# Hybrid decoder step on one core: token lists taken ahead of the sums, the turning and the down products; the samples' output projection stacked

## What is computed

```
z = h @ w_in                                   # four mixer branches and their gates
merged = sum_k sigmoid(gate_k) * (branch_k @ w_branch[k])
x = x + gate1 * (merged @ w_out)               # output projection
h = rmsnorm(x) * (1 + scale2) + shift2
scores = sigmoid(h @ router_w)                 # 64 experts, top 8 of each token
hg, hu = h @ e_gate[e], h @ e_up[e]            # 1024 -> 256, for each expert e
act = silu(hg) * hu * gates[:, e]
routed = sum_e act @ e_down[e]                 # 256 -> 1024
shared = (silu(h @ s_gate) * (h @ s_up)) @ s_down
x = x + gate2 * (routed + shared);  y = rmsnorm(x, final_g)
```

## Time and profile before

| what | value |
|---|---|
| median of 3 runs | 928.19 us |
| profiled execution: time, span | 926.03 us, 924.3 us |
| granted TensorE clock, mean | 0.988 |
| PE busy | 863.1 us (93% of the span) |
| DVE busy | 565.5 us (61%) |
| ACT busy | 308.5 us (33%) |
| DMA | 295.80 MB, mean 320 GB/s |
| longest group of PE | L870, 128x264, 1024 of them, 192.6 us |

### The profile page before, as it was taken

How to read it: one execution, slowest core, us unless ns; L and a number is a source line. 1 busy time by engine, 2 the same in 40 slices (tenths; PEclk the granted TensorE clock), 3 DMA queues, 4 the chain that set the end, 5 groups by cost and what they waited for, 6 DMA issues and landing times.

```text
span 924.3 us, 21357 instructions
## 1 busy us (share of the span) xinstructions
PE 863.1 (93%) x7880; PEld 647.2 (70%) x7880; DVE 565.5 (61%) x1415; ACT 308.5 (33%) x583; POOL 48.7 (5%) x89
## 2 busy tenths in 40 slices
PE   4799999999999998999898999999999999999995
PEld 2699999999999897566665556556665655665562
DVE  2557988899986667456354545446454654555455
ACT  3555444344346241122222323232222323222323
POOL 2010000000000000000000000000000000000000
PEclk9999999999999999999899999999999999999998
DMA  9985557888777628899988999999999999999911
GB/s 341 334 248 151 180 179 273 270 300 285 247 248 272 207 83 348 341 389 371 401 327 343 400 396 405 418 404 405 422 409 411 413 419 408 413 414 420 408 49 49
DMA packets 92702, 295.80 MB, mean 320 GB/s; under 512 B 7718, under 2 KB 45670, under 8 KB 67659
## 3 DMA queue, kind: packets, MB, share of 16 engines
q1 hardware_dynamic: 86139, 280.55, 79.3%
q0 software_dynamic: 6016, 13.10, 3.8%
q10 hardware_dynamic: 489, 1.33, 0.4%
HBM read 300.19 MB, written 4.14 MB: 329 GB/s over the span
## 4 chain that ended last, share of the span: by engine, by line
PE 67%; DMA 16%; DVE 8%; issue 5%; ACT 2%; SPq 0%; DVEq 0%; POOLq 0%; ACTq 0%
PE psum L870 26%; DMA xn<-h_table,idx 13%; PE psum L1310 7%; PE psum L1268 6%; PE psum L1227 5%; PE psum L874 5%; PE psum L1222 4%; PE psum L1259 3%; PE psum L913 2%; PE psum L1225 2%; PE psum L1228 2%; DMA wexp<-in_ada_w 1%; DMA wexp<-in_w_in 1%; DVE bc_r L2203 1%; PE psum L1274 1%
## 5 line engine op out<-in xcount | busy, mean ns | idle before, releaser
L870 PE MATMUL psum<-xn_r,wexp_r 128*128 128x264 f32 x1024 | 192.6, 287 | 7.5 <-DVE hT_r L1804 5.9
L870 PEld LDWEIGHTS psum<-xn_r,wexp_r 128*128 128x128 f32 x1024 | 160.5, 189 | 10.2 <-issue 7.8
L870 PE MATMUL psum<-hT_r,wexp_r 128*128 128x264 f32 x512 | 145.5, 284 | 0.0
L1766 DVE TENSOR_TENSOR wexp_r<-wexp,wexp_r 128x1024 fp32r<-128x1024 f32 x88 | 106.5, 1216 | 20.9 <-ACT wexp_r L1482 20.4
L1482 ACT ACTIVATE wexp_r<-wexp 128x1024 fp32r<-128x1024 f32 x88 | 92.3, 1054 | 60.2 <-PE psum L870 44.4
L1225 PE MATMUL psum<-wexp,mid 128*128 128x512 f32 x240 | 108.8, 599 | 0.8 <-ACT mid L1626 0.8
L2203 DVE TENSOR_TENSOR bc_r<-psum,xn_r 32x256 fp32r<-32x256 f32 (+2 forms) x140 | 67.6, 483 | 51.5 <-ACT xn_r L1659 28.2
L2188 DVE SCALAR_TENSOR_TENSOR hT<-psum,gcol,hT 128x256 f32<-128x256 f32 (+2 forms) x64 | 26.3, 411 | 116.8 <-ACT hT L1642 116.6
L870 PEld LDWEIGHTS psum<-hT_r,wexp_r 128*128 128x128 f32 x512 | 97.1, 190 | 0.1
L870 PE MATMUL psum<-wexp_r 128*128 128x264 f32 (+2 forms) x576 | 82.4, 283 | 1.4 <-DVE wexp L2014 1.4
L1225 PEld LDWEIGHTS psum<-wexp,mid 128*128 128x128 f32 x240 | 43.3, 190 | 57.6 <-issue 56.3
(11 more groups left out here) (329 smaller groups left out, 1291.0 us busy)
## 6 DMA issues: line engine op xcount, KB each, us to landing
wexp<-in_e_gate SPq DMA_DIRECT2D x64, 1024.0 KB, 8.2
wexp<-in_e_up SPq DMA_DIRECT2D x64, 1024.0 KB, 10.6
wexp<-in_e_down SPq DMA_DIRECT2D x64, 1024.0 KB, 9.7
wexp<-in_w_in SPq DMA_DIRECT2D x32, 1024.0 KB, 6.0
mid<-in_ada_w SPq DMA_DIRECT2D x8, 2048.0 KB, 9.7
wexp<-in_w_branch SPq DMA_DIRECT2D x8, 1024.0 KB, 5.4
wexp<-in_ada_w SPq DMA_DIRECT2D x14, 512.0 KB, 10.4
wexp<-in_w_out SPq DMA_DIRECT2D x4, 1024.0 KB, 5.8
```

Of the source, the lines that this page charges most:

```text
L870: last = mm(out, a[x], b[y], start=start and x == y == 0, stop=stop and x == 1)
L1766: V.tensor_tensor(as_r(low(u, q)), low(u, q), as_r(high(u, q)).bitcast(F32), ALU.subtract).then_inc(S["w_lo"], 1)
```

## The change

It makes these edits (cut to the core). The hunks are, in this order: the bank order, the banks of the sums, `mix` on PE, the turning of the second gate (`gateT`), the waits of `turn_rows`, `up` and `sums`, `last_sums`, and the bodies of PE and of DVE.

```
-        if (t, j) == (0, 1):
+        if (t, j) == (1, 0):
             out += [("h2T", 2, h) for h in range(2)]
...
+SUM_BANKS = (5, 6, 0, 5, 6, 0, 5, 0)
...
+        m_samples = poolH.rearrange(...)[:, 0:KT * (SAMPLE_TILE + NS)].rearrange("p (k m) -> p k m", k=KT)
...
+        def sum_ahead(c):
+            return max((b + 1 for b in range(c) if SUM_BANKS[b] == SUM_BANKS[c]), default=0)
...
+                if t == 2:
+                    both = psum[0:SAMPLE_TILE + NS, ...]
+                    for k in ks:
+                        if (j, h) == (0, 0):
+                            pe.wait_ge(S["m_split"], k + 1)
+                        if k:
+                            mm(out, as_r(m_samples[:, k, 0:NS]), w[1][:, k], start=False, stop=False)
+                        last = mm(both, as_r(m_samples[:, k, :]), w[0][:, k], start=(k == 0), stop=(k == KT - 1))
...
+            out = claim("gateT")
+            for c in range(KT):
+                last = turn(out[...], mod[:, 3 * D + c * P:3 * D + (c + 1) * P], NC_ROWS)
...
-                need(pe, S["sum_taken"], KT * sums)
+                need(pe, S["sum_taken"], KT * sums - 1)
...
-                        pe.wait_ge(S["sum_taken"], KT * sums_before(i, j) - 2)
+                        pe.wait_ge(S["sum_taken"], KT * sums_before(i, j))
...
-                    if c > 2:
-                        pe.wait_ge(S["sum_taken"], KT * i + c - 2)
+                    if sum_ahead(c):
+                        pe.wait_ge(S["sum_taken"], KT * i + sum_ahead(c))
...
+                down(LAST, UNROLL - 1)
                 last_sum(0, 1, 1)
-                down(LAST, UNROLL - 1)
+                turn_samples()
...
-                    up(i, j, range(4))
...
+                    if not prev:
+                        up(i, j, range(2))
...
                         token_list(0, 2)
+                        up(i, j, range(2, 4))
+                        turn_rows(0, 1, 0)
+                        up(i, j, range(4, 6))
                         token_list(0, 3)
+                        up(i, j, range(6, KT))
+                    else:
+                        up(i, j, range(4))
+                        turn_act(pi, pj)
+                        up(i, j, range(4, KT))
+                    if not last:
+                        token_list(i + 1, j)
                     if sums_at(i, j):
                         sums(i)
...
                     gated(i, j)
+                    if not last:
+                        list_out(i + 1, j)
```

More of the change, by code:

```diff
@@ L92, in jobs_of_mixer @@
         out.append(("mix", t, j))
-        if (t, j) == (0, 1):
+        if (t, j) == (1, 0):
             out += [("h2T", 2, h) for h in range(2)]
-    out += [("h2T", 0, h) for h in range(2)] + ["logit_first"] + [("h2T", MIX_ORDER[-1], h) for h in range(2)]
+    out += [("h2T", 0, h) for h in range(2)] + ["logit_first", "gateT"] + [("h2T", MIX_ORDER[-1], h) for h in range(2)]
     out += ["logit", ("shared_gate", 0), ("shared_up", 0), ("shared_gate", 1), ("shared_up", 1), "sort_turn", "sort", "slot", "order", "lists"]
@@ L1068, in mix @@
                 out = psum[0:n, bank_of(("mix", t, j))[0], h * UNIT:(h + 1) * UNIT].rearrange("p (q n) -> p q n", q=2)
+                if t == 2:
+                    both = psum[0:SAMPLE_TILE + NS, bank_of(("mix", t, j))[0], h * UNIT:(h + 1) * UNIT].rearrange("p (q n) -> p q n", q=2)
+                    for k in ks:
[4 more added lines that the diff above has]
+                        last = mm(both, as_r(m_samples[:, k, :]), w[0][:, k], start=(k == 0), stop=(k == KT - 1))
+                        if not k:
+                            last = mm(out, as_r(m_samples[:, k, 0:NS]), w[1][:, k], start=False, stop=False)
+                    return last
                 for k in ks:
-                    if (t, j, h) == (2, 0, 0):
-                        pe.wait_ge(S["m_split"], k + 1)
                     last = mm3(out, [as_r(m_hi[:, k, t0:t0 + n]), as_r(mT[:, k, t0:t0 + n])], [x[:, k] for x in w], start=(k == 0), stop=(k == KT - 1))
@@ L1100, in _ @@
             full(logits(out, MIX_ORDER[1], range(KT)), "logit_first")
+            await_freed(pe, ("ada", 11))
+            out = claim("gateT")
+            for c in range(KT):
+                last = turn(out[:, c * NC_ROWS:(c + 1) * NC_ROWS], mod[:, 3 * D + c * P:3 * D + (c + 1) * P], NC_ROWS)
+            full(last, "gateT")
             turn_h(MIX_ORDER[2])
@@ L1198, in _ @@
             await_freed(pe, ("shared_gate", 1))
[L1200 to L1205, removed]
             def up(i, j, ks):
@@ L1381, in body @@
                         down(pi, pj)
[L1382 to L1385, removed]
                     if last and j == 2:
@@ L1617, in _ @@
             scores("logit", MIX_ORDER[2:])
+            b = await_full(ac, "gateT")
+            free(F(gate_col[:], b[:, 0:KT * NC_ROWS].rearrange("p (c r) -> p c r", r=NC_ROWS)[:, :, NS], ACT.Copy), "gateT")
             def shared_silu(j):
@@ L2043, in _ @@
                 a = slice(j * BLK, (j + 1) * BLK)
-                free(V.tensor_tensor(xn[0:n, t, a], b[0:n, :], rows_of(0, t, n, a.start, a.stop), ALU.mult), ("mix", t, j))
+                if t == 2:
+                    link(V.tensor_copy(xn[0:n, t, a], b[SAMPLE_TILE:SAMPLE_TILE + n, :]))
+                    link(V.tensor_tensor(xn[0:n, t, a], b[0:n, :], xn[0:n, t, a], ALU.add))
+                    free(V.tensor_tensor(xn[0:n, t, a], xn[0:n, t, a], rows_of(0, t, n, a.start, a.stop), ALU.mult), ("mix", t, j))
+                else:
+                    free(V.tensor_tensor(xn[0:n, t, a], b[0:n, :], rows_of(0, t, n, a.start, a.stop), ALU.mult), ("mix", t, j))
                 await_freed(ve, ("mix", t, j))
@@ L2146, in list_out @@
                     ve.wait_ge(S["act_ready"], e - 3)
+                    if j == 1 and light_group(i - 1) and not light_group(i):
+                        ve.wait_ge(gathered[buffer_of(i - 1, 1)], 16 * (i + 1))
                 if first_group(i) and j < FIXED:
@@ L2285, in body @@
                         take_tokens(i)
+                    if first and j == 0:
+                        ve.wait_ge(S["token_taken"], 1)
+                        rows_unused(0)
+                        link(rows_unused(1))
                     if not last:
@@ L2302, in body @@
                         rows_out(*next_sheet(i, j))
-                    if first and j == 0:
-                        ve.wait_ge(S["token_taken"], 1)
-                        rows_unused(0)
-                        link(rows_unused(1))
-                    if not last and j == UNROLL - 1:
-                        list_out(i + 1, j)
                     if last and j:
@@ L2312, in body @@
                         y_out(pi, pj)
-                    if not last and j < UNROLL - 1:
-                        list_out(i + 1, j)
-                    if gate_columns_at(i, j):
-                        gate_columns()
                     if last and j == 1:
@@ L2320, in body @@
                         rows_beyond()
[L2322 to L2325 removed]
             def gate_sums():
[L2329 removed]
+                await_freed(ve, "gateT")
                 ve.wait_ge(S["sum_taken"], KT * (LAST + 1))
```

37 lines of the change are left out of this document (14 added, 23 removed).

## The result

| | before | changed |
|---|---|---|
| median of 20 runs each | 927.81 us | 931.87 us |
| ratio | | 1.0057, 95% interval 1.0045 to 1.0069 |
| profiled execution: span | 924.3 us | 928.8 us |
| granted clock, mean | 0.988 | 0.985 |
| PE busy | 863.1 us | 862.9 us |

What follows compares the result with a forecast made beforehand. PE was taken as the bound, waiting mainly for gathers, not DMA. +6 - 4.2 - 1.1 - 3.8 + 1.7 - 0.7 - 1.5 - 1.7 = -5.3 on 926.0 gave 920.7, plus 1.0: 921.7 us, range 912 to 928.

Steps and rivals of the forecast that it cites:

- Step 1: Loop groups 4 to 14: 22 new mask waits of 0.74, +16.3, less 10.4 of gather waits; net rounded to +6.
- -0.1: In the loop, the turning no longer waits for the last sums' bank: 0.1 us gained.
- The 10.4 us: PE's gather waits in loop groups 4 to 14, once a group, counted as coming back, about 0.5 staying in group 4.
- Step 2: Samples' output projection: 32 products fewer, -3.6, and an earlier start, -0.6; -4.2 in all, bounds -3.3 and -5.
- Step 3: Job (0, 0): up(0, 1) no longer waits 0.78 for ACT's rows and sums(0) starts a little sooner; -1.1.
- Step 4: Group 1: the 3.39 gather wait and slow clock behind it go, against new mask waits; -3.8, then +1.7.
- +1.7: Group 1: the clock falls behind the new 2.77 us wait for mask (2, 0), costing 1.7 us.
- Steps 5 and 6: Groups 2 and 3: -0.7 and -1.5; last group, gather wait gone and last down moved ahead: -1.7.
- The rivals: Other outcomes: masks earlier than thought, chance 0.18; no change, 0.26; slower, 0.06; clock holds in group 1, 0.10.
- The slower one: Rival: loop masks wait for a y_out whose ACT copy comes late, 1.3 us a wait; over 933 to 936, chance 0.06.

Runs made afterwards that it cites:

- g2: Changed kernel with masks early and old banks, plus list 3's mask right behind list 2's and the token maps behind a group's last list_out: 899.39 us, ratio 0.9723.

## Why the prediction was wrong

**What bounds the kernel**: right. Gathers and masks were what PE waits for, DMA was not the bound. g2's 420 GB/s shows it.

**Step 1, the loop: +6 forecast for eleven groups, +16.0 measured** in ten periods of 1.1 to 3.2 us more each. This is the step that failed, in the price of a new mask wait. Where it waits was right: at jobs 1 and 3 of each group, 16.9 us against 16.3, and the gathers' waits went. What it had wrong:
- The price of the list at its new place. I took the 0.16 us behind a down with me, and 0.06 from the mask to PE. Both are figures of other places: the 0.06 is that of a written-out group, where the list then takes 0.22; in the loop a list that starts with its mask starts 0.14 behind it and takes 0.58 or more. The trace of the kernel before had this already, at 673.52; I read PE's row ahead of it (672.41) and not the next one.
- The stretches. By the forecast, down to sums would be 3.70 + 0.74 and down to turning 3.72 + 0.71; measured are 4.99 and 5.15, so 1.3 us a group more. About 0.5 of that comes back, because list (i+1, 3) had cost 0.58 behind the turning and list (i+1, 0), now there, costs 0.08.
- The banks: I wrote -0.1 for the turning that no longer waits. The measured price is +0.4 us a group, 5 us in all. I looked at the wait that the edit took away and not at the one that it brought, block 7 behind block 5.
- The clock. I had waits of 0.7 cost nothing beyond themselves. The profile shows two falls in the loop of 1.65 us each, at job 3, where list and turning stand idle 1.08 + 0.18.
- Job 3's wait was 1.08, not 0.71: list_out(i+1, 2) now stands ahead of that `y_out`, 0.15 us, PE arrives 0.1 sooner without a list behind its down, and the mask takes 0.08 more to reach it. Job 1's was 0.52, not 0.74, since PE came to it 0.34 later than forecast; of that, `up` began 0.20 late.
- The gathers. The 10.4 us are eleven waits, the longest of which, 2.06, and one of 0.75 fall ahead of the ten periods; 8.0 could be won in them.

Of the 16.0, then, by the stretches: 12.9 from down to sums and 14.3 from down to turning, together with 16.4 of mask waits; 0.9 in the sums; less 15.0 from turning to turning, of which 8.0 are gather waits and 5.0 the list that left; and 3.3 for the clock. The rest of that 15.0, some 2, I didn't trace. Against the kernel before, the sums lost only these 0.9, since DVE's additions now begin 0.77 behind their start (618.32 to 619.09) where it was 1.18 (656.88 to 658.06); with the old banks and the moved lists they take 3.98 where they took 4.19.

**Step 2, the projection, -4.2**: right. The 32 products bring 3.4 to 3.6 from the first product to the end, and the first product comes 0.85 sooner (28.08 against 28.92 behind L913), more than the 0.6 taken: 4.2 to 4.4 in all. The last addition starts at 337.48 and not at 335.9 only because this profile was 1.8 late from before.

**Step 3, job (0, 0), -1.1**: the two traces show 2.6 us gained ahead of group 0 and 3.2 at 387.47 against 390.66, so 0.6. No run tested it.

**Step 4, group 1, -3.8 and +1.7**: the wait of 3.39 and the slow clock behind it went, mask (2, 0) cost 2.73 as against 2.77 forecast. The clock is the open part: behind that same wait, 2.70 to 2.74 long in seven profiles, it fell in four and held in three, the first among them. From that list to the next turning it is 11.7 us (12.4 with the old banks) where the clock held and 13.3 to 14.5 where it fell, 1.6 to 2.8 more. So +1.7 is right about half of the time, and in the first profile it didn't come. By the rule of the Trainium skill ("HAM oscillation — how this bites in real kernels", in TensorE: Matmul & The Clock Gate) only longer gaps bring the clock down; the four falls here and those behind 1.1 us don't agree with it.

**Steps 5 and 6**: from 442.61 to 555.88 5.1 us were gained, against 4.7 forecast for groups 2 and 3 and for group 1's slow clock, which lies behind 442.61 (0.7 + 1.5 + 2.45); the stretch also holds most of group 4, so this tests no term by itself. The tail brought 1.4 to 1.6 against 1.25 for the down, and its gather wait of 0.47 went.

**The reading of the earlier trace rows**: sums that are not yet added were not next after the gathers. The wait of 1.94 for ACT's rows at the end, used in step 6, is longer; nothing in the sum hangs on it.

**The rivals.** The slower one was the right side, from another cause than I gave: not ACT's copy, which is on time (`y_out` begins 1.90 behind down at job 1, 1.89 before), but the list in the loop, the banks and the clock. I priced a wait by its length alone; the forecast's sign hung on one term of 22 equal parts, and 0.24 us more on each turns it. The range was too narrow for that.

## What to carry to other kernels

When work is moved ahead on one engine, move ahead on the other what it waits for: the change as it was costs 4 to 5 us; with the masks early it gains 16, and with the old banks and the token maps moved as well 26 (the projection's 4 in each). Where a new wait is repeated in a loop, price it by everything between its neighbours' starts, not by the wait, take that price from a row of the same loop and not of a group written out, and give the range that error times the count. When two profiles are compared by start times, look first how far apart they are ahead of the first edit; here that was 1.8 us, as much as a whole step of the forecast. And try each small part that goes with a change alone: the banks, which looked like a relief, cost as much as the whole change did.

## What the hardware showed that I had not expected

TensorE's clock falls to 1.2 GHz (granted 0.50) behind idle times of 1.1 us, once or twice in a run of eleven groups with the same waits, each time for about 1.65 us of lost time. Behind one and the same wait of 2.7 us it fell in four of seven profiles; the three in which it held had waits of 2.71 to 2.74, the four others 2.70 to 2.71. In the kernels without those waits (masks early) the groups show no fall at all. The length of a wait alone doesn't decide it. And three small bf16 products, over in 0.16 to 0.26 us when their mask is early and in 0.22 behind a wait of up to 2.73 in the written-out groups, take 0.58 in the loop when they start with their mask, after a wait of 1.1 us and after none alike.
